# Joint accumulation of a modulation vector in a two-block transformer kernel, with its sums at two seams

## The reference, cut to what matters

```python
c_act = silu(c)
mod = (c_act @ w_ada + b_ada)            # w_ada: 2048 x 12288
sh1, sc1, g1, sh2, sc2, g2 = split(mod, 6)
h = rms_norm(x, norm_mix) * (1 + sc1) + sh1
x = x + g1 * hybrid_mixer(h, w_in, w_out, ...)
h = rms_norm(x, norm_ffn) * (1 + sc2) + sh2
x = x + g2 * conv_glu_ffn(h, w_ffn_up, ..., w_ffn_down)
return rms_norm(x, norm_final)
```

## Time and profile before

| what | value |
|---|---|
| runs | 2350.42, 2351.67, 2352.06 us |
| the profiled execution | 2352.51 us, its span 2350.7 us |
| TensorE busy | 2337.8 us (99%) |
| VectorE busy | 1616.4 us (69%) |
| ScalarE busy | 1153.2 us (49%) |
| HBM | 535 MB read, 230 GB/s over the span |

### The profile page before, as it was taken

How to read it: one execution, slowest core, us unless ns; L and a number is a source line. 1 busy time by engine, 2 the same in 40 slices (tenths; PEclk the granted TensorE clock), 3 DMA queues, 4 the chain that set the end, 5 groups by cost and what they waited for, 6 DMA issues and landing times.

```text
span 2350.7 us, 43754 instructions
## 1 busy us (share of the span) xinstructions
PE 2337.8 (99%) x17937; PEld 2151.6 (92%) x17937; DVE 1616.4 (69%) x1931; ACT 1153.2 (49%) x1510; POOL 5.1 (0%) x7
## 2 busy tenths in 40 slices
PE   9999999999999999999999999999999999999998
PEld 8889778999999999888999899888999999998887
DVE  5668568777777766877778455667878666665556
ACT  5565454534344344444764444546544445454444
POOL 0000000000000000000000000000000000000000
PEclk9999999999999999999999999999999999999999
DMA  8556567888888877898577545555778656665563
GB/s 308 167 179 197 159 234 271 278 282 297 282 282 295 282 242 263 316 324 315 175 279 269 163 130 153 196 200 187 283 255 295 208 179 206 196 206 197 192 192 117
DMA packets 233049, 543.62 MB, mean 231 GB/s; under 512 B 15610, under 2 KB 22596, under 8 KB 232260
## 3 DMA queue, kind: packets, MB, share of 16 engines
q1 hardware_dynamic: 232756, 540.97, 68.3%
q10 hardware_dynamic: 144, 0.52, 0.1%
HBM read 535.11 MB, written 6.32 MB: 230 GB/s over the span
## 4 chain that ended last, share of the span: by engine, by line
PE 98%; DVE 0%; ACT 0%; issue 0%; DMA 0%; SPq 0%; DVEq 0%; ACTq 0%
PE ps L330 37%; PE ps L1858 18%; PE ps L608 18%; PE ps L2216 16%; PE ps L1875 2%; PE ps L2509 0%; PE ps L1041 0%; PE ps L1053 0%; PE ps L1071 0%; PE ps L1083 0%; PE ps L2141 0%; PE ps L460 0%; PE ps L2744 0%; PE ps L1134 0%; PE ps L2921 0%
## 5 line engine op out<-in xcount | busy, mean ns | idle before, releaser
L297 DVE TENSOR_TENSOR weights_lo<-raw_weights,weights_hi 128x1024 fp32r<-128x1024 f32 x786 | 957.6, 1224 | 659.8 <-ACT weights_hi L289 658.0
L289 ACT ACTIVATE weights_hi<-raw_weights 128x1024 fp32r<-128x1024 f32 x782 | 827.2, 1062 | 1086.8 <-PE ps L330 446.4
L516 DVE SCALAR_TENSOR_TENSOR ada_acc<-ada_w,col,ada_acc 128x1024 f32<-128x1024 f32 x180 | 230.2, 1279 | 0.1
L330 PE MATMUL ps<-conv_x_hi,weights_hi 128*128 128x256 f32 x1280 | 198.0, 277 | 0.0
L330 PE MATMUL ps<-glu_x_hi,weights_hi 128*128 128x256 f32 x1280 | 197.7, 276 | 0.0
L330 PE MATMUL ps<-glu_x_hi,weights_lo 128*128 128x256 f32 x1280 | 197.2, 276 | 0.0
L330 PE MATMUL ps<-glu_x_lo,weights_hi 128*128 128x256 f32 x1280 | 197.2, 276 | 0.0
L330 PE MATMUL ps<-conv_x_lo,weights_hi 128*128 128x256 f32 x1280 | 197.2, 276 | 0.0
L330 PE MATMUL ps<-conv_x_hi,weights_lo 128*128 128x256 f32 x1280 | 197.2, 276 | 0.0
L330 PEld LDWEIGHTS ps<-conv_x_hi,weights_hi 128*128 128x128 f32 x1280 | 169.1, 188 | 1.0 <-issue 1.0
L330 PEld LDWEIGHTS ps<-glu_x_hi,weights_hi 128*128 128x128 f32 x1280 | 169.0, 188 | 0.0
(11 more groups left out here) (560 smaller groups left out, 3635.3 us busy)
## 6 DMA issues: line engine op xcount, KB each, us to landing
raw_weights<-in_w_in_dram SPq DMA_DIRECT2D x202, 512.0 KB, 5.0
ada_w<-in_w_ada_dram SPq DMA_DIRECT2D x96, 1024.0 KB, 6.1
raw_weights<-in_w_ffn_up_dram SPq DMA_DIRECT2D x176, 512.0 KB, 4.6
raw_weights<-in_w_gate_dram SPq DMA_DIRECT2D x88, 512.0 KB, 4.6
raw_weights<-in_w_up_dram SPq DMA_DIRECT2D x88, 512.0 KB, 4.6
raw_weights<-in_w_down_dram SPq DMA_DIRECT2D x88, 512.0 KB, 5.7
raw_weights<-in_w_ffn_down_dram SPq DMA_DIRECT2D x88, 512.0 KB, 4.3
raw_weights<-in_w_out_dram SPq DMA_DIRECT2D x64, 512.0 KB, 5.1
```

What stands on the lines that cost most here:

```text
L289: kit.nc.scalar.activation(kit.slots(n, i)[0], raw, ACT.Copy).then_inc(kit.w_hi, 1)
L297: kit.nc.vector.tensor_tensor(lo, raw, hi.bitcast(F32), ALU.subtract).then_inc(kit.w_lo, 1)
L330: ins = nc.tensor.matmul(out, lhsT=lhsT, rhs=rhs, start=start and m == 0, stop=(k == KT - 1 and m == 2), skip_group_check=True)
L516: step = nc.vector.scalar_tensor_tensor(acc, w, c, acc, ALU.mult, ALU.add)
```

## The change

1. Groups 0 to 7 are accumulated jointly. A copy brings 16 rows of all eight groups, and partition 16 g + r holds row r of group g (`Ada.source`). 128 such steps go into one accumulator instead of 16 steps into each of eight. Groups 8 and 9 go the same way with 64 rows of two groups per copy (32 steps into one accumulator). Each copy has 512 KB, so there are two for each 1 MB of before. Groups 10 and 11 keep their shape.
2. The sums of groups 0 to 7 are eight products with a mask of eight columns at the first seam, those of 8 and 9 eight products with a mask of two columns at the second. `turn_sums`, `reduce_sums`, `last_scales`, the waits on them, and one of the two trips of accumulators through DRAM are gone.
3. The first seam gets eight filler transposes behind `turn_early`; the second has eleven instead of three.
4. The rows of groups 10 and 11 are summed with a rounded block of ones and the accumulator split in high and low part: four fp32r products per group instead of two float32 products.
5. c is needed with partition p holding element p mod 16 (and p mod 64) of each step. So there are two more small vectors, three more small copies, one more pack, a broadcast copy and one more Silu.
6. In Down the final norm's weight (1 MB) is loaded at k = 12 instead of at the start. In Glu VectorE copies 16 columns of c per group. At the seams VectorE makes all of the stage's modulation scales before 1/rms.

The diff, cut to its core:

```diff
@@ class Ada
+    def source(self, lead, j, s):
+
+        w = self.kit.ins["w_ada_2"][0]
+        if lead < 8:
+            rows = w[ds(OCT * (16 * lead + s) + 16 * OCT * j, OCT), 0:16 * UN]
+        elif lead < 10:
+            rows = w[HALF * (16 * (lead - 8) + s):HALF * (16 * (lead - 8) + s + 1), 16 * UN:20 * UN]
+        else:
+            rows = w[P * s:P * (s + 1), 2 * UN * lead:2 * UN * (lead + 1)]
+        return rows.rearrange("r (g n) -> g r n", n=2 * UN)
...
-        sp.dma_start(self.w[:, m % 2, :, :], w[2 * m * P:2 * (m + 1) * P, ds(2 * UN * lead + 2 * UN * j, 2 * UN)]
-                     .rearrange("(k p) n -> p k n", p=P)).then_inc(kit.ada_w[m % 2], 16)
+        for s in (2 * m, 2 * m + 1):
+            sp.dma_start(self.w[:, m % 2, s % 2, :], self.source(lead, j, s)).then_inc(kit.ada_w[m % 2], 16)
...
+        if s == 0 and lead in (0, 8, 10, 11):
+            step = nc.vector.tensor_scalar(acc, w, c, None, ALU.mult)
+        else:
             dve.wait_ge(kit.ada_acc, 16 * lead + s + 16 * j)
-            step = nc.vector.scalar_tensor_tensor(acc, w, c, acc, ALU.mult, ALU.add)
-        else:
-            step = nc.vector.tensor_scalar(acc, w, c, None, ALU.mult)
+            step = nc.vector.scalar_tensor_tensor(acc, w, c, acc if prior is None else prior, ALU.mult, ALU.add)
...
+    def sums(self, pe, bank, mask, acc):
+
+        kit, (a, b) = self.kit, self.kit.at[mask]
+        n = b - a
         for q in range(8):
-            step = nc.tensor.matmul(kit.ps[:, bank, q:q + 1], lhsT=self.acc[:, q * P:(q + 1) * P],
-                                    rhs=kit.c("ones")[:, 0:1], start=True, stop=True)
+            step = kit.nc.tensor.matmul(kit.ps[:, bank, n * q:n * (q + 1)], lhsT=acc[:, q * P:(q + 1) * P],
+                                        rhs=kit.c(mask), start=True, stop=True)
...
+    def summed(self, lead, bank, mask):
+
+        kit, (a, b) = self.kit, self.kit.at[mask]
+        n, first, bias = b - a, 8 * lead, COLS["b_ada_2"] + 8 * lead
+        cols, add = (x.rearrange("p (g q) -> p q g", q=8) for x in (kit.modcols[:, first:first + 8 * n],
+                                                                    kit.col[:, bias:bias + 8 * n]))
+        return kit.nc.vector.tensor_tensor(cols, kit.ps[:, bank, 0:8 * n].rearrange("p (q g) -> p q g", g=n), add, ALU.add)
@@ FirstMixer: columns of c
+        if n == len(self.packs) - 2:
+            dve.wait_ge(self.s_packs, 16 * sum(len(p[0]) for p in self.packs[1:]))
+            self.kit.nc.vector.tensor_copy(self.pack[:, 0, :].rearrange("p (g r) -> p g r", r=OCT),
+                                           self.c_rows[:, :].unsqueeze(1).broadcast_to([P, P // OCT, OCT])
+                                           ).then_inc(self.s_cwide, 1)
@@ Glu
-            mid = (lambda: self.ada.turned(pe, self.lead, j)) if summed else None
-                if summed and s == begun:
-                    self.ada.reduced(dve, self.lead, j)
+                    q = 8 * half + s // 2
+                    if q == 0:
+                        a = COLS["c_oct"] + 16 * self.lead
+                        dve.wait_ge(kit.ada_acc, 16 * self.lead + 16 * j)
+                        nc.vector.tensor_copy(self.c_turn[:, :], kit.col[:, ds(a + 16 * j, 16)]).then_inc(self.s_c, 1)
+                        dve.wait_ge(self.s_c, 1 + j)
+                    self.ada.product(dve, self.lead, j, q, c=self.c_turn[:, q:q + 1])
@@ Down
-        sp.wait_ge(kit.ada_sum, self.lead)
-        sp.dma_start(self.final_w[:, :], self.final_src).then_inc(kit.loaded, 16)
+                if k == 12:
+                    sp.wait_ge(kit.ada_acc, 16 * self.lead + 1)
+                    self.load_final(sp)
-            if p == 0 and begun:
-                pe.wait_ge(kit.ada_out, self.lead)
+    def ada_sums(self, pe):
+
+        pe.wait_ge(self.kit.ada_acc, 128)
+        self.ada.sums(pe, 0, "oct", self.accs[0])
+
+    def ada_summed(self, dve):
+
+        dve.wait_ge(self.kit.ada_sum, 1)
+        self.ada.summed(0, 0, "oct").then_inc(self.kit.ada_out, 1)
+        dve.wait_ge(self.kit.ada_out, 1)
@@ SecondMixer
-        self.down.ada_sums(pe, 0)
-        self.down.ada_sums(pe, 1, 0, 2)
+        self.down.ada_sums(pe)
         pe.wait_ge(self.squares_in, 11)
         for k in range(4):
             self.turned.turn_early(pe, k)
-        self.down.ada_sums(pe, 1, 2, 8)
+        keep_busy(kit, 8, 7, S)
...
+        self.down.ada_summed(dve)
         modulation(kit, 0)
-        sp.dma_start(self.mem["acc_dram"].ap()[0], self.down.accs[2]).then_inc(self.s_accout, 16)
@@ ConvGlu
+        self.ada.sums(pe, 1, "half", self.mixer.acc_back)
-        turn_sums(kit, mixer.accs[:, 1, :], 2).then_inc(kit.ada_sum, 1)
...
-                keep_busy(kit, 3, 7, S)
+                keep_busy(kit, 11, 7, S)
...
-        self.first_scales(dve)
+        self.scales(dve)
...
-        modulation(kit, 1, 0, 8)
+        modulation(kit, 1)
...
-                            self.last_scales(dve)
+        pe.wait_ge(self.s_acclo, g + 1)
+        for b in range(2):
+            for acc in (self.acc_hi, self.acc_lo):
+                step = nc.tensor.matmul(kit.ps[:, 4 + 2 * g + b, :], lhsT=self.ones[:, :], rhs=acc[:, b * UN:(b + 1) * UN],
+                                        start=acc is self.acc_hi, stop=acc is self.acc_lo)
+                    g = self.acc_split(i, j, u, 1)
+                    if g is not None:
+                        act.wait_ge(kit.ada_acc, 16 * (self.lead + g + 1))
+                        if g == 0:
+                            nc.scalar.activation(self.ones[:, :], kit.c("ones"), ACT.Copy)
+                        else:
+                            act.wait_ge(kit.ada_sum, 2 + g)
+                        nc.scalar.activation(self.acc_hi[:, :], self.ada.acc, ACT.Copy).then_inc(self.s_acchi, 1)
+                    g = self.acc_split(i, j, u, 3)
+                    if g is not None:
+                        dve.wait_ge(self.s_acchi, g + 1)
+                        nc.vector.tensor_tensor(self.acc_lo[:, :], self.ada.acc, self.acc_hi[:, :].bitcast(F32), ALU.subtract
+                                                ).then_inc(self.s_acclo, 1)
```

More of the change, by code:

```diff
@@ L153, in __init__ @@
             self.sem(n) for n in ("weights_hi", "weights_lo", "act_hi", "act_lo"))
-        self.ada_w = [self.sem("ada_w0"), self.sem("ada_w1")]
+        self.ada_w = [self.sem(f"ada_w{n}") for n in range(2)]
         self.ada_acc, self.ada_sum, self.ada_out = (self.sem("ada_" + n) for n in ("acc", "sum", "out"))
@@ L454, in spread @@
     return kit.nc.tensor.transpose(out, col.broadcast_to([P, P]), kit.c("ident"))
[L457 to L468, removed]
@@ L503, in product, with scalar @@
+    def scalar(self, lead, s):
+        name, first = ("c_oct", 0) if lead < 8 else ("c_half", 8) if lead < 10 else ("c_2", lead)
+        return self.kit.cols(name, 16 * (lead - first) + s)
+    def product(self, dve, lead, j, s, acc=None, prior=None, c=None):
         nc, kit = self.kit.nc, self.kit
         m, k = s // 2, s % 2
[L505 to L509, removed]
@@ L944, in turn_pack @@
         _, w, _ = self.packs[n]
-        kit.nc.tensor.transpose(kit.ps[:, 6, 0:w], self.pack[0:w, n, :], kit.c("ident")[0:w, 0:w]
-                                ).then_inc(self.s_packT, 1)
+        last = n == len(self.packs) - 1
+        if last:
+            pe.wait_ge(self.s_cwide, 1)
+        rows = self.pack[0:w, 0 if last else n, :]
+        kit.nc.tensor.transpose(kit.ps[:, 6, 0:w], rows, kit.c("ident")[0:w, 0:w]).then_inc(self.s_packT, 1)
     def spread_scale(self, at):
@@ L3574, in __init__ @@
             kit.sem("conv_" + n) for n in ("taps", "base", "sums", "silu", "glu"))
-        self.s_gate, self.s_scales = kit.sem("gate2_bias_in"), kit.sem("last_scales")
+        self.s_gate = kit.sem("gate2_bias_in")
+        self.acc_hi, self.acc_lo = (t(f"ada_acc_{n}", at, [P, 2 * UN], R32) for n, at in (("hi", 60), ("lo", 64)))
+        self.ones = t("ones_rounded", 92, [P, P], R32)
+        self.s_acchi, self.s_acclo = (kit.sem(n) for n in ("ones_and_ada_acc_hi", "ada_acc_lo"))
         self.down = None
@@ L3610, in scale_sums @@
     def scale_sums(self, pe):
-        kit, mixer = self.kit, self.mixer
-        pe.wait_ge(mixer.s_accs, 16)
-        pe.wait_ge(kit.pair_free[0], self.uses[0] + 1)
-        for q in range(8):
-            step = kit.nc.tensor.matmul(kit.ps[:, 1, q:q + 1], lhsT=mixer.accs[:, 0, q * P:(q + 1) * P],
-                                        rhs=kit.c("ones")[:, 0:1], start=True, stop=True)
-        step.then_inc(kit.ada_sum, 1)
-        pe.wait_ge(mixer.s_xlast, ST)
-        turn_sums(kit, mixer.accs[:, 1, :], 2).then_inc(kit.ada_sum, 1)
@@ L3622, in first_scales @@
[L3622 to L3639 removed]
+        pe.wait_ge(self.mixer.s_accs, 16)
@@ L3648, in row_sums, with acc_split @@
         step.then_inc(kit.ada_sum, 1)
+    def acc_split(self, i, j, u, after):
```

(2 more changed lines are left out.)

185 lines of the change are left out of this document (66 added, 119 removed).

## The result

The kernel after takes 2821.77 us (median of four runs, 2795.92 to 2845.37) against 2351.82: the ratio is 1.196, 95% interval 1.187 to 1.206. The kernel is 20% slower, 470 us above the forecast of 2342.9 and outside the range, on the side of rival 1, and beyond that rival's 2641 as well.

A forecast was written before the change was run, and what follows sets the result against it. TensorE was taken as the bound, busy 2337.8 of 2350.7 us. Terms -5.2, -1.6, -2.4, +0.1 and +0.3 summed to -8.8, giving 2342.9 us (own range 2341 to 2347); the eight-in-ten range was 2341 to 2680.

The forecast's parts named there:

- rival 1: Modulation copies run on only as many DMA engines as they have outermost blocks: +253 to +343, 2641 us; chance 0.41.
- The transfers (part 1): Modulation weight loads: new copies run like the old ones, cost 0 at the lower bound.
- The sign that the prediction named: TensorE showing waits over 1 us outside of the seams would mean the forecast is wrong.
- groups 8 and 9: Down and SecondMixer: two-block copies on two engines, +124 to +153 for group 8 and +120 to +150 for group 9.
- groups 0 to 7 on eight engines: Eight-block copies: groups 6 and 7 in Down +9 to +29, Glu 0 to +11.
- fewer than about six engines: Group 8's stretch in Down turns slow once fewer engines than this carry a two-block copy; 74 us for 5.1 MB each.
- rival 3: Only the eight-block copies suffer, or the tight first mixer stalls: +9 to +40, 2365 us; chance 0.04.
- The sums inside Glu: In Glu, six pieces of eight transposes, 0.87 us each, leave TensorE's chain: -5.2 us.
- The gate rows: Row sums of groups 10 and 11: four fp32r products replace two float32 products, 0.91 for 1.72 us, twice: -1.6.
- The first seam: Between Down and SecondMixer: fewer narrow products, earlier scaling and fillers holding the clock, -2.4 us, bounds -2.6 and -0.6.
- The small vectors: Early loading of c: one more pack, a broadcast copy and three small issues on SyncE, +0.3 us, bounds 0.1 and 1.5.
- Rival 2: At the seams, fillers don't hold TensorE's clock: first seam gains 0.6 instead of 2.4, second may lose 2.3; 2346 us; chance 0.08.

The follow-up runs named there:

- e9_plain: The kernel after, but its modulation copies bring 128 rows of one group as before, still two of 512 KB per buffer: 2343.65 us, ratio 0.9965.
- e3_half2: The kernel after, with only the copies of groups 0 to 7 put rows outermost (16 blocks); groups 8 and 9 keep two blocks: 2690.12 us, ratio 1.144.
- e1_spread: The kernel after, with groups 0 to 7 copied rows outermost (16 blocks) and copies of groups 8 and 9 cut in two of 64 rows: 2429.73 us, ratio 1.033.
- e12_blocks8: The kernel before, with two 512 KB modulation copies for each 1 MB, each read as eight blocks of 16 rows: 2663.47 us, ratio 1.132.
- e2_oct8: The kernel after, with only the copies of groups 8 and 9 cut in two of 64 rows; groups 0 to 7 keep eight blocks: 2592.85 us, ratio 1.102.
- e6_blocks16: The kernel before, with two 512 KB modulation copies for each 1 MB, each read as 16 blocks of eight rows: 2411.62 us, ratio 1.030.
- e11_plain_few: The kernel after with plain 128-row copies, without the eight fillers at the first seam and with three instead of eleven at the second: 2345.06 us, ratio 0.9972.
- e8_cols512: The kernel before, with each 1 MB modulation copy made four of 256 KB, each to all 128 partitions with 512 columns: 2352.31 us, ratio 1.001.
- e10_joined: The kernel before, with the fp32r gate rows and, at the first seam, four fillers ahead of group 7's products with a column of ones: 2351.03 us, ratio 0.9995.

## Why the prediction was wrong

- **The transfers (part 1), 0.** This is the step that failed: "The sum holds only if the new copies run like the old ones", with the value at its lower bound. They do not: fewer engines carry them, and a packet takes longer. From e9_plain to the kernel after it is 469 us. The sign that the prediction named came true: TensorE waits for the splits for up to 18.4 us outside of the seams.
- **The choice between the bounds.** The nearest rows were taken to be the large copies of 128 rows, though the new copies share their size and not the property in question. The rows of small copies and the Trainium skill's rule that rival 1 cites both pointed to the other end. They could not price it, but they spoke for more than the 0.41 that it got.
- **Rival 1, groups 8 and 9, +244 to +303.** Right in size and in mechanism: 260 by e3_half2 less e1_spread. Against plain copies it may be more: e3_half2's Down and SecondMixer are 296 us longer than e9_plain's, with the loss of groups 6 and 7 in it. Only the landing was put too short, 10 to 20 us for a copy, where a pair takes 35 to 38.
- **Rival 1, groups 0 to 7 on eight engines, +9 to +40; "fewer than about six engines".** Wrong by far. The six are a slip: by the prediction's own figures each of k engines has 8.4 / k + 0.9 MB to move in 74 us at 22.5 to 25.7 GB/s, which takes about 9 to 11 engines. e12_blocks8 and e2_oct8 show that eight are too few for this kernel. The larger error was the engine's rate. In Glu after, 41.9 MB of modulation weights pass in the 559 us from the first product of the five groups to the last, 75 GB/s, and the other 146 of the 221 GB/s are spread. An engine of the eight then moves 75 / 8 + 146 / 16 = 18.5 GB/s and is busy nearly all the time (by the packets' mean times for 539 of the 559 us), not 22.5 to 25.7. Those rates were measured on plain copies. In an eight-block copy a packet of 4 KB takes longer even while nothing else moves: 211 ns with eight in flight (after, 600 to 1000), where a plain copy's takes 160 with 16 in flight (e9_plain, 600 to 880).
- **A second fault that no case of the prediction had.** The shape alone, on sixteen engines, costs 86 us (e1_spread less e9_plain) and 60 (e6_blocks16). 86 + 163 + 260 = 509, more than the measured 469; why the parts don't add up was not tested. The loss in FirstMixer, 22 us, is not of this kind: e2_oct8 has it (449.9) and e1_spread hasn't (422.9), so it belongs to the eight-block copies, and rival 3 alone had named that stage.
- **The sums inside Glu, -5.2.** Measured 480.2 for 485.9, -5.7.
- **The gate rows, -1.6.** 0.92 us for 1.72, twice; the stretch to the end -1.5. Right.
- **The first seam, -2.4.** 8.1 for 10.5. Right, and by its working: scaling begins at 1146.26, and the unit ends 4.9 us later, forecast 5.0. **The second, +0.1.** +0.15.
- **The small vectors, +0.3.** +1.0 in e9_plain, +0.4 in e11_plain_few; inside the bounds.
- **Rival 2, the fillers don't hold the clock.** Refuted at both seams. But they are worth 0.8 us at the first, not 1.8: e11_plain_few has 1.7 of that seam's 2.4 without them, with eight narrow products fewer than before.
- **Rival 3, eight-block copies, +9 to +40.** Its first half happened, at six times the highest price: 249 us by e2_oct8 less e9_plain, the fault of the shape in it.

## What to carry to other kernels

When a change reshapes a copy, price the copy before the compute: count the blocks of its outermost dimension on both sides, since eight and two of them ran on eight and two of the sixteen DMA engines here, and keep the partitions in one plain dimension of 128, since two dimensions over them, or 64 of them, made the whole kernel 2.5 to 4% longer here even with sixteen blocks or more. Here a low DMA share beside a wait for data (0.34) went with too few engines, and a high share at a low rate (0.95 at 269 GB/s) with such a shape. A term whose bounds are 0 and +300 us deserves more thought than all terms of microseconds, however well these are worked out.

## What the runs showed that was not expected

- SyncE is held too while it issues these copies (it may be that the queue is full; no row shows that). The issues of `ada_w` after, where before had a median of 373 ns and a longest of 1252:

```profile
L487 SPq DMA_DIRECT2D ada_w<-in_w_ada_dram x192: 340/640/12952, 324.5 to 2302.3; - x192
```

- Four times as many copies, of 256 KB instead of 1 MB, cost nothing (e8_cols512, 0 to 0.2%).
- Filler transposes held 2.4 GHz through a seam with an idle gap of 0.6 us (e9_plain, granted clock 1.00), and four of them amid 32 records of single-column products didn't (e10_joined, 0.50).
